# Norm statistics laid out on 128 tokens instead of four column strips (RMS norms) and at full width (layer norms)

## The chip, the cores and the metric

The program runs on one core of a Trainium2 chip. The metric is the device time of one execution in microseconds (us). The core has a matrix engine (PE; its weight loads are listed as PEld), a vector engine (DVE), an activation engine (ACT), a general engine (POOL) and a queue engine (SP) that starts the weight transfers. All data are float32.

## The reference, cut to what matters

The input is a sequence of 512 tokens of width 1024. Two blocks follow each other. The first puts 16 learned tokens in front (528 in all) and normalises four times with a layer norm; the second works on 512 tokens and normalises eight times with an RMS norm:

```
def layer_norm(x, g, b):
    mu = jnp.mean(xf, axis=-1, keepdims=True)
    var = jnp.mean(jnp.square(xf - mu), axis=-1, keepdims=True)
    y = (xf - mu) * lax.rsqrt(var + LN_EPS)
    return y * g + b

def _rmsnorm(x, g):
    y = xf * lax.rsqrt(jnp.mean(xf * xf, axis=-1, keepdims=True) + NORM_EPS)
    return y * g

# first block, 2 layers:   h = layer_norm(ALPHA * h + mixer(h), ...);  h = layer_norm(ALPHA * h + conv_ffn(h), ...)
# second block, 2 layers:  x = x + _rmsnorm(mixer(_rmsnorm(x, g0)), g1);  x = x + _rmsnorm(conv_ffn(_rmsnorm(x, g2)), g3)
```

## The kernel before, in words

Activations lie with the width on the 128 partitions and the tokens along the free axis, as eight tiles of 128 x 528 (or 128 x 512). X is the residual, Z the stream, A the activations. So the mean over the width of one token is a sum over partitions and over eight tiles. The kernel takes it with matmuls against MEANW, a tile filled with 1/1024.

The five engines run programs of their own and meet through semaphores. The order of the work is written out by hand: `when(name, what, n)` gives the semaphore and the value at which the n-th result `what` of the norm `name` is there. In the order of the program the norms are

- lru, ffn0, fox, ffn1: centred (layer norm), 528 tokens, each on the sum of a projection and the residual;
- mixin: RMS, on the residual, at the start of the second block;
- mix, ffn2, gla, ffn3: "out" norms (RMS), on the output of a projection (`rms_out`, which also adds the result to X);
- ffn2in, glain, ffn3in: "in" norms (RMS), on the residual that the out norm has just updated (`rms_in`). ffn2in follows mix, glain follows ffn2, ffn3in follows gla.

A norm has these steps. ACT squares the eight tiles (L2395, in an out norm L2384, where POOL has already added up the first four squares in NORM_MU, so that PE reads five tiles and not eight). PE waits for each square and multiplies it. Before, `squares_of` (L2236) splits the tokens into four strips of 132 or 128; strip g goes with 32 columns of MEANW into rows 32g to 32g+31 of one PSUM bank, four matmuls per tile. ACT takes the root of this 128 x 132 (or 128 x 128) tile (L2397), DVE its reciprocal (L2625), and PE spreads the four strips over all partitions again with four matmuls of one row each (L2250) into four banks. DVE then multiplies the eight tiles by the gain and by these roots in PSUM (L2619 in a layer norm, L2631 in an in norm, L2644 in an out norm). In a layer norm ACT adds the bias and writes X (L2401).

What waits on whom around a norm: the matmuls behind it start with the first normalised tile. POOL's weight combinations of ffn0, ffn1, ffn2 and ffn3 (L2817 to L2825) start as soon as the last centred tile (layer norm) or the last updated X tile (out norm) is there, so for lru, fox, ffn2in and ffn3in they run beside the norm. In ffn2in and ffn3in DVE also makes the combinations of the moving operand (L2543 to L2551) after the multiplications, then two memsets that ACT waits for.

Of the kernel before, what the change touches and what calls it, by code (L numbers as in the profile page):

```python
# [110 lines left out]
def build(nc, x_t, units, cols, gate_w2, out):  # L111
    ctx = ExitStack()
    with ctx:
# [45 lines left out]
        def parts(T):  # L159
            return [(0, 0, HALF), (1, HALF, HALF)] if T == T1 else [(0, 0, T)]  # L160
# [25 lines left out]
        def S(name):  # L186
            if name not in sems:
# [9 lines left out]
        PER = {"mean": 1, "mu": 1, "ctr": KD, "sc": KD, "sq": KD, "zsum": SUMS - 1, "sqsum": SUMS - 1, "var": 1, "std": 1, "rec": 1, "spread": 1, "x": KD,  # L197
               "pad": 1, "tap": 2 * NF, "conv": 2 * NF, "gelu": NF, "act": NF}

        def shared(what, name):  # L200
            return S(("ffn_" if what in ("pad", "tap", "conv", "gelu", "act") else "norm_") + what)

        def when(name, what, n):

            order = (FFNS if what in ("pad", "tap", "conv", "gelu", "act") else SUMMED if what == "sqsum" else
                     NORMS)
            return shared(what, name), n + PER[what] * order.index(name) + (what in ("conv", "act"))

        def credit(eng, *names):
# [2 lines left out]
                eng.sem_inc(S(name), 1)  # L212

        def mean_squares(T):
            return PS[:, 1, 0:T // 4]

        def roots(T):
            return NORM_R[:, 0:T // 4]  # L220

        def root_banks(name):
            return 2 if name == "ffn0" else 4

        def spread_roots(name, T):
            return PS[:, root_banks(name):root_banks(name) + 4, 0:T // 4]

        def by_quarter(ap):
            return ap.rearrange("p (g t) -> p g t", g=4)

        def at_k(name, what):
            return shared(what, name), lambda k: when(name, what, k + 1)[1]
# [1865 lines left out]
        def _(pe):  # L2098
# [118 lines left out]
            def norm(name, T, centred, summed=False):  # L2217

                if centred:

                    pe.wait_ge(tile_free, BUFS + {"lru": TILES["ffn0"], "ffn0": TILES["fox_f"], "fox": TILES["ffn1"], "ffn1": TILES["ssd_pre"]}[name])

                    pe.wait_ge(*when(name, "zsum", SUMS - 1))
                    for b, t, n in parts(T):
                        nc.tensor.matmul(PS[:, 6 + b, 0:n], MEANW[:, 0, :], NORM_MU[:, t:t + n], start=True, stop=False)
                    for k in range(SUMS, KD):
                        pe.wait_ge(q_added, z_ready(name, k))
                        for b, t, n in parts(T):
                            mm = nc.tensor.matmul(PS[:, 6 + b, 0:n], MEANW[:, 0, :], Z[:, k, t:t + n], start=False, stop=(k == KD - 1))
                    mm.then_inc(shared("mean", name), 1)  # L2230
                n = T // 4

                def squares_of(k, tile):
# [4 lines left out]
                    return mm  # L2238

                if summed:  # L2240
                    pe.wait_ge(tile_free, BUFS + {"mix": TILES["ffn2"], "ffn2": TILES["gla_pre"], "gla": TILES["ffn3"], "ffn3": TILES["end"]}[name])
                    pe.wait_ge(*when(name, "sqsum", SUMS - 1))
                    squares_of(0, NORM_MU[:, 0:T])
                for k in range(SUMS if summed else 0, KD):
                    pe.wait_ge(*when(name, "sq", k + 1))
                    mm = squares_of(k, scratch(SQ_AT, KD, T2)[:, k, :] if summed else A[:, k, 0:T])
                mm.then_inc(shared("var", name), 1)
                pe.wait_ge(*when(name, "rec", 1))
                for g in range(4):
                    mm = nc.tensor.matmul(spread_roots(name, T)[:, g, :], ONES[32 * g:32 * g + 1, :], roots(T)[32 * g:32 * g + 1, :],  # L2250
                                          start=True, stop=True)
                mm.then_inc(shared("spread", name), 1)

            def ffn(n, T, h, before):
                name = f"ffn{n}"
# [81 lines left out]
        def _(act):  # L2337
# [48 lines left out]
            def norm(name, T, src, centred, ready, ready_n, eps):  # L2386
                if centred:
                    act.wait_ge(*when(name, "mean", 1))
                    nc.scalar.activation(sv(NORM_MU[:, 0:T], T), ps_tile(6, T), ACT.Copy).then_inc(shared("mu", name), 1)

                spare = 96 + NORMS.index(name)
                nc.scalar.activation(SMALL[:, spare:spare + 1], SMALL[:, eps:eps + 1], ACT.Sqrt)
                for k in range(KD if ready else 0):
                    act.wait_ge(ready, ready_n(k))
                    nc.scalar.activation(A[:, k, 0:T], src(k), ACT.Square).then_inc(shared("sq", name), 1)  # L2395
                act.wait_ge(*when(name, "var", 1))
                nc.scalar.activation(roots(T), mean_squares(T), ACT.Sqrt, bias=SMALL[:, eps:eps + 1]).then_inc(shared("std", name), 1)  # L2397
# [120 lines left out]
        def _(dve):  # L2518
# [92 lines left out]
            def ln(name, g, k0):  # L2611
                dve.wait_ge(*when(name, "mu", 1))
                for k in range(KD):
                    dve.wait_ge(q_added, z_ready(name, k))
                    v.tensor_tensor(Z[:, k, :], Z[:, k, :], NORM_MU[:, :], ALU.subtract).then_inc(shared("ctr", name), 1)
                reciprocal_roots(name, T1)
                for k in range(KD):
                    dve.wait_ge(*when(name, "ctr", k + 1))
                    v.scalar_tensor_tensor(out=by_quarter(Z[:, k, :]), in0=by_quarter(Z[:, k, :]), scalar=col(g, k0 + k),  # L2619
                                           in1=spread_roots(name, T1), op0=ALU.mult, op1=ALU.mult).then_inc(shared("sc", name), 1)  # L2620

            def reciprocal_roots(name, T):

                dve.wait_ge(*when(name, "std", 1))
                v.reciprocal(roots(T), roots(T)).then_inc(shared("rec", name), 1)  # L2625
                dve.wait_ge(*when(name, "spread", 1))

            def rms_in(name, g, into=None):
                reciprocal_roots(name, T2)
                for k in range(KD):  # L2630
                    v.scalar_tensor_tensor(out=by_quarter(Z[:, k, 0:T2]), in0=by_quarter(X[:, k, META:T1]), scalar=col("norm_g", g * 8 + k),  # L2631
                                           in1=spread_roots(name, T2), op0=ALU.mult, op1=ALU.mult).then_inc(shared("x", name), 1)
                    if into is not None and k == KD // 2 - 1:
                        dve.wait_ge(*when(name, "x", KD // 2))
                        moving(CHUNKS[into], 1, KD // 2, lambda k0, k1, a, z: Z[:, k0:k1, a:z], T2 // 2, T2)
                if into is not None:
                    dve.wait_ge(*when(name, "x", KD))
                    for m in range(2, 5):
                        moving(CHUNKS[into], m, KD // 2, lambda k0, k1, a, z: Z[:, k0:k1, a:z], T2 // 2, T2)

            def rms_out(name, g):
                reciprocal_roots(name, T2)
                for k in range(KD):
                    c(v.scalar_tensor_tensor(out=by_quarter(Z[:, k, 0:T2]), in0=by_quarter(Z[:, k, 0:T2]), scalar=col("norm_g", g * 8 + k),  # L2644
                                             in1=spread_roots(name, T2), op0=ALU.mult, op1=ALU.mult))
# [386 lines left out]
```

## Time and profile before

| | us |
|---|---|
| median of 3 runs (3443.97 to 3451.95) | 3444.69 |
| the profiled execution's own time | 3444.69 |
| its span, first to last instruction | 3443.0 |
| PE busy in the span | 3272.9 (95%) |
| DVE / ACT / POOL busy | 1685.1 / 1029.8 / 1138.7 |
| share of PE in the chain that ended last | 88% |

### The profile page before, as it was taken

To read this page: it belongs to the slowest core of one execution; us is meant where nothing else is said; L and a number is where in the kernel's file an instruction comes from. 1 tells how busy PE (TensorE), PEld (TensorE's weight loads), DVE (VectorE), ACT (ScalarE), POOL (GpSimd) and SP (SyncE) were. 2 spreads that over 40 slices of the span, in tenths; PEclk is the share of its full clock that TensorE was granted. 3 is DMA by queue.
4 is the path that set the end of the run, shared out by engine and by line. 5 is a ranking of instruction groups with operands and counts; after the bars stand their busy time and mean duration, and the time that the engine had idled before them with its cause. 6 is when DMAs were issued, how large, how long until landed. Compare 5 with 4: busy or idle time off the path is not lost.

```text
span 3443.0 us, 51186 instructions
## 1 busy us (share of the span) xinstructions
PE 3272.9 (95%) x16742; PEld 2647.2 (77%) x16742; DVE 1685.1 (49%) x2837; ACT 1029.8 (30%) x2083; POOL 1138.7 (33%) x920
## 2 busy tenths in 40 slices
PE   9999999989999999998999999989999899799997
PEld 7787888867776788886446787868888588688886
DVE  3454546454445354644546545354553534355544
ACT  3433232122332223212317333122321334222311
POOL 0024444432221344442001333344444222353543
PEclk9999999999999999997999999989999899899999
DMA  3222222211111122221210211212222221122222
GB/s 119 82 83 92 79 91 79 92 68 50 56 50 38 68 79 91 79 92 49 68 55 21 67 55 55 70 65 91 79 92 80 67 68 62 49 73 89 88 89 76
DMA packets 68669, 249.35 MB, mean 72 GB/s; under 512 B 7568, under 2 KB 7568, under 8 KB 68544
## 3 DMA queue, kind: packets, MB, share of 16 engines
q1 hardware_dynamic: 68544, 247.72, 20.9%
q8 instruction: 74, 1.21, 0.1%
q14 instruction: 51, 0.42, 0.0%
HBM read 245.59 MB, written 2.10 MB: 72 GB/s over the span
## 4 chain that ended last, share of the span: by engine, by line
PE 88%; DVE 6%; ACT 3%; issue 2%; DVEq 0%; POOL 0%; DMA 0%; ACTq 0%; SPq 0%; POOLq 0%
PE psum L2188 54%; PE psum L2123 10%; PE psum L431 6%; PE psum L1742 3%; PE psum L1300 3%; PE psum L1327 1%; PE psum L1767 1%; PE psum L463 1%; PE psum L2288 1%; PE psum L1354 1%; PE psum L501 1%; DVE residual L2646 1%; DVE stream L2644 1%; ACT scratch L1033 1%; PE psum L485 1%
## 5 line engine op out<-in xcount | busy, mean ns | idle before, releaser
L2188 PE MATMUL psum<-scratch 128*128 128x256 f32 (+1 forms) x3600 | 817.1, 383 | 11.3 <-POOL scratch L2820 5.8
L2188 PEld LDWEIGHTS psum<-scratch 128*128 128x128 f32 x3600 | 684.8, 190 | 119.4 <-ACT scratch L2354 7.9
L2817 POOL TENSOR_TENSOR scratch<-w_ring 128x512 f32<-128x512 f32 (+2 forms) x160 | 201.7, 1261 | 1366.1 <-DMA w_ring<-units 806.3
L2354 ACT ACTIVATE scratch<-psum 128x264 f32<-128x264 f32 (+1 forms) x480 | 184.5, 386 | 889.8 <-PE psum L2188 863.1
L2669 DVE TENSOR_TENSOR scratch<-scratch,psum 128x264 f32<-128x264 f32 (+1 forms) x264 | 108.3, 424 | 502.9 <-PE psum L2188 475.0
L2188 PE MATMUL psum<-scratch,w_ring 128*128 128x256 f32 (+1 forms) x1200 | 275.6, 382 | 0.0
L2188 PEld LDWEIGHTS psum<-scratch,w_ring 128*128 128x128 f32 x1200 | 227.9, 190 | 34.9
L2188 PE MATMUL psum<-acts,w_ring 128*128 128x264 f32 (+1 forms) x1088 | 247.8, 386 | 2.6 <-ACT scratch L2469 1.1
L2188 PEld LDWEIGHTS psum<-acts,w_ring 128*128 128x128 f32 x1088 | 208.0, 192 | 35.9 <-issue 2.6
L2417 ACT ACTIVATE scratch<-scratch,params 128x528 f32<-128x528 f32 (+1 forms) x176 | 144.4, 821 | 274.9 <-DVE scratch L2669 274.9
L2822 POOL TENSOR_TENSOR scratch<-w_ring 128x512 f32<-128x512 f32 (+2 forms) x160 | 225.9, 1412 | 0.0
L2825 POOL TENSOR_TENSOR scratch<-w_ring,scratch 128x512 f32<-128x512 f32 (+2 forms) x160 | 224.7, 1405 | 2.9 <-PE psum L2188 2.9
L2820 POOL TENSOR_TENSOR scratch<-scratch,w_ring 128x512 f32<-128x512 f32 (+2 forms) x160 | 219.5, 1372 | 12.5
L2676 DVE SCALAR_TENSOR_TENSOR scratch<-scratch,params 128x528 f32<-128x528 f32 (+1 forms) x176 | 201.6, 1145 | 25.5 <-DVE scratch L2674 9.0
L2674 DVE SCALAR_TENSOR_TENSOR scratch<-scratch,params 128x528 f32<-128x528 f32 (+1 forms) x176 | 204.2, 1160 | 0.0
L2123 PE MATMUL psum<-residual,w_ring 128*128 128x264 f32 (+1 forms) x800 | 181.1, 389 | 6.2 <-DMA residual<-x_t 6.2
L2123 PE MATMUL psum<-stream,w_ring 128*128 128x512 f32 (+1 forms) x400 | 179.6, 604 | 1.0 <-DVE stream L2631 1.0
L2123 PEld LDWEIGHTS psum<-residual,w_ring 128*128 128x128 f32 (+1 forms) x800 | 149.5, 188 | 37.3 <-issue 8.2
L2188 PE MATMUL psum<-residual,w_ring 128*128 128x264 f32 x704 | 165.3, 394 | 3.5 <-ACT residual L2401 3.5
L2188 PE MATMUL psum<-stream,w_ring 128*128 128x256 f32 x704 | 159.9, 386 | 1.9 <-DVE stream L2631 1.9
L2188 PEld LDWEIGHTS psum<-residual,w_ring 128*128 128x128 f32 x704 | 137.0, 195 | 28.2 <-issue 3.9
L2188 PEld LDWEIGHTS psum<-stream,w_ring 128*128 128x128 f32 x704 | 136.6, 194 | 21.7 <-issue 2.5
(456 smaller groups left out, 4760.3 us busy)
## 6 DMA issues: line engine op xcount, KB each, us to landing
w_ring<-units SPq DMA_DIRECT2D x463, 512.0 KB, 3.6
residual<-x_t SPq DMA_DIRECT2D x4, 528.0 KB, 6.5
out_t<-residual SPq DMA_DIRECT2D x4, 512.0 KB, 2.7
params<-cols SPq DMA_DIRECT2D x1, 568.5 KB, 8.5
gate_w_sb<-gate_w SPq DMA_DIRECT2D x1, 96.0 KB, 10.5
```

What stands on the lines that cost most here:

```text
L431: mm = nc.tensor.matmul(fx_bank(p), weights(k), moving(k), start=(p in (1, 2, 5) and k == 0), stop=(k == 3), skip_group_check=True)
L2123: mm = nc.tensor.matmul(PS[0:m1 - m0, bank + b, 0:n], W[:, s, q, m0:m1], rhs(k)[:, t:t + n], start=(k == 0), stop=(k == slots[-1][1] + slo ...
L2188: mm = nc.tensor.matmul(out, weights(k), moving(k), start=(p in (1, 2, 5) and k == 0), stop=(k == h - 1), skip_group_check=(p != 2))
L2354: nc.scalar.activation(kept(q, n, H), quad_bank(q, p, H), ACT.Copy).then_inc(q_copied, 1)
L2417: nc.scalar.activation(y[:, j, 0:T], xp[:, j, 0:T], ACT.Identity, bias=w(3), scale=w(0)).then_inc(shared("tap", name), 1)
L2669: v.tensor_tensor(xp[:, row, at:at + H], kept(q, keep, H), quad_bank(q, p, H), ALU.add).then_inc(q_added, 1)
L2674: c(v.scalar_tensor_tensor(out=y[:, j, 0:T], in0=xp[:, j, 1:1 + T], scalar=PAR[:, ds(w0 + 1, 1)], in1=y[:, j, 0:T], op0=ALU.mult, op1=ALU. ...
L2676: v.scalar_tensor_tensor(out=y[:, j, 0:T], in0=xp[:, j, 2:2 + T], scalar=PAR[:, ds(w0 + 2, 1)], in1=y[:, j, 0:T], op0=ALU.mult, op1=ALU.ad ...
L2817: g.tensor_tensor(s(1), row(1, 0), row(1, 1), ALU.add).then_inc(q_weight, 1)
L2820: g.tensor_tensor(s(2), s(1), row(0, 0), ALU.subtract).then_inc(q_weight, 1)
L2822: g.tensor_tensor(s(3), row(0, 0), row(1, 0), ALU.subtract).then_inc(q_weight, 1)
L2825: g.tensor_tensor(s(4), row(0, 1), s(2), ALU.subtract).then_inc(q_weight, 1)
```

## The change

RMS norms (512 tokens). The squares become the stationary operand: for each block of 128 tokens, `squares_of` multiplies the 128 x 128 block of squares with one column of MEANW, so that the mean of token p of block j stands in row p of column j. The result is 128 x 4, added over the tiles. ACT takes the root of 128 x 4, DVE its reciprocal (into SMALL), and then DVE makes four diagonal matrices (identity times one column of roots, "diag"), and PE multiplies them with ONES into one bank, which gives the roots of 512 tokens on all partitions. The multiplications read this bank.

Layer norms (528 tokens). PE multiplies each square with all 128 columns of MEANW in two halves of 264 tokens, so that all partitions hold the variance. ACT takes the root of 128 x 528, DVE the reciprocal of 128 x 528 in SBUF, and the multiplications read that. There is no spreading matmul.

```
-                for g in range(4):
-                    mm = nc.tensor.matmul(mean_squares(T)[32 * g:32 * g + 32], MEANW[:, 0, 0:32], tile[:, n * g:n * g + n],
-                                          start=(k == 0), stop=(k == KD - 1), skip_group_check=True)
...
-                pe.wait_ge(*when(name, "rec", 1))
-                for g in range(4):
-                    mm = nc.tensor.matmul(spread_roots(name, T)[:, g, :], ONES[32 * g:32 * g + 1, :], roots(T)[32 * g:32 * g + 1, :], start=True, stop=True)
+                if T == T2:
+                    def squares_of(k, tile):
+                        for j in range(T2 // P):
+                            mm = nc.tensor.matmul(rms_v[:, j:j + 1], tile[:, P * j:P * j + P], MEANW[:, 0, 0:1], start=(k == 0 and j == 0), stop=True, skip_group_check=True)
...
+                    for j in range(T2 // P):
+                        pe.wait_ge(*when(name, "diag", j + 1))
+                        mm = nc.tensor.matmul(rms_r[:, P * j:P * j + P], ONES[:, :], NORM_R[:, P * j:P * j + P], start=True, stop=True)
...
+                for k in range(KD):
+                    pe.wait_ge(*when(name, "sq", k + 1))
+                    for b, t, n in parts(T):
+                        mm = nc.tensor.matmul(PS[:, 6 + b, 0:n], MEANW[:, 0, :], A[:, k, t:t + n], start=(k == 0), stop=(k == KD - 1))
...
-                nc.scalar.activation(roots(T), mean_squares(T), ACT.Sqrt, bias=SMALL[:, eps:eps + 1])
+                if T == T2:
+                    nc.scalar.activation(rms_t, rms_v, ACT.Sqrt, bias=SMALL[:, eps:eps + 1])
+                    return
+                nc.scalar.activation(sv(NORM_R[:, 0:T], T), ps_tile(6, T), ACT.Sqrt, bias=SMALL[:, eps:eps + 1])
...
+                c(v.reciprocal(NORM_R[:, :], NORM_R[:, :]))
...
-                    v.scalar_tensor_tensor(out=by_quarter(Z[:, k, :]), in0=by_quarter(Z[:, k, :]), scalar=col(g, k0 + k), in1=spread_roots(name, T1), ...)
+                    v.scalar_tensor_tensor(out=Z[:, k, :], in0=Z[:, k, :], scalar=col(g, k0 + k), in1=NORM_R[:, :], ...)
...
+            def rms(name):
+                dve.wait_ge(*when(name, "std", 1))
+                c(v.reciprocal(rms_t, rms_t))
+                for j in range(T2 // P):
+                    v.tensor_scalar(NORM_R[:, P * j:P * j + P], ID[:, :], rms_t[:, j:j + 1], None, ALU.mult).then_inc(shared("diag", name), 1)
+                dve.wait_ge(*when(name, "spread", 1))
```

On PE, at the norms ffn1 (a layer norm) and mixin (an RMS norm), which follow each other, the program has before (the size is the rows and columns of the output):

```order
L2229 MATMUL psum<-stream,mean_weights 128x264 x8
L2236 MATMUL psum<-acts,mean_weights 32x132 x32
L2250 MATMUL psum<-norm_r,ones 128x132 x4
L2236 MATMUL psum<-acts,mean_weights 32x128 x32
L2250 MATMUL psum<-norm_r,ones 128x128 x4
L789 MATMUL psum<-w_ring,stream 128x64 x32
```

and after the change:

```order
L2215 MATMUL psum<-stream,mean_weights 128x264 x8
L2241 MATMUL psum<-acts,mean_weights 128x264 x16
L2221 MATMUL psum<-mean_weights,acts 128x1 x32
L2235 MATMUL psum<-norm_r,ones 128x128 x4
L775 MATMUL psum<-w_ring,stream 128x64 x32
```

The layer norm has sixteen matmuls of 264 columns for its 32 short ones and no spreading matmuls; the RMS norm has as many matmuls as before, each of one column with a new 128 x 128 stationary operand.

On PE, at the norms mix (out) and ffn2in (in), between the projection and the next feed-forward part, the program has before:

```order
L2236 MATMUL psum<-norm_mu,mean_weights 32x128 x4
L2236 MATMUL psum<-scratch,mean_weights 32x128 x16
L2250 MATMUL psum<-norm_r,ones 128x128 x4
L2236 MATMUL psum<-acts,mean_weights 32x128 x32
L2250 MATMUL psum<-norm_r,ones 128x128 x4
```

and after the change:

```order
L2221 MATMUL psum<-mean_weights,norm_mu 128x1 x4
L2221 MATMUL psum<-mean_weights,scratch 128x1 x16
L2235 MATMUL psum<-norm_r,ones 128x128 x4
L2221 MATMUL psum<-mean_weights,acts 128x1 x32
L2235 MATMUL psum<-norm_r,ones 128x128 x4
```

Nothing has changed its place; the forms have changed.

On DVE, at ffn1 and mixin, before:

```order
L2615 TENSOR_TENSOR stream<-stream,norm_mu 128x528 x8
L2625 RECIPROCAL norm_r<-norm_r 128x132
L2619 SCALAR_TENSOR_TENSOR stream<-stream,params,psum 128x528 x8
L2625 RECIPROCAL norm_r<-norm_r 128x128
L2631 SCALAR_TENSOR_TENSOR stream<-residual,params,psum 128x512 x8
```

and after the change:

```order
L2608 TENSOR_TENSOR stream<-stream,norm_mu 128x528 x8
L2610 RECIPROCAL norm_r<-norm_r 128x528
L2613 SCALAR_TENSOR_TENSOR stream<-stream,params,norm_r 128x528 x8
L2619 RECIPROCAL small<-small 128x4
L2621 TENSOR_SCALAR norm_r<-identity,small 128x128 x4
L2627 SCALAR_TENSOR_TENSOR stream<-residual,params,psum 128x512 x8
```

The layer norm's reciprocal is four times as wide and its multiplications read no PSUM; the RMS norm's reciprocal has four columns, and four operations that build diagonals stand behind it.

## Rows read from the trace of the kernel before

**Rows 1.** The page: the span, and the chain that ended last by engine.

```profile
span 3443.0 us, 51186 instructions
...
PE 88%; DVE 6%; ACT 3%; issue 2%; DVEq 0%; POOL 0%; DMA 0%; ACTq 0%; SPq 0%; POOLq 0%
```

**Rows 2.** Timeline of the norm lru: start, duration, engine, line, operation, count, idle before.

```profile
297.24 3.72 PE L2229 MATMUL psum<-stream,mean_weights 128*128 128x264 f32 x16
...
303.71 4.42 PE L2236 MATMUL psum<-acts,mean_weights 128*32 128x132 f32 x64 [2.75 <-ACT acts L2395]
...
308.19 0.37 ACT L2397 ACTIVATE norm_r<-psum,small 128x132 f32<-128x132 f32 x1 [0.79 <-PE psum L2236]
...
308.60 0.98 DVE L2625 RECIPROCAL norm_r<-norm_r 128x132 f32<-128x132 f32 x1 [1.92 <-ACT norm_r L2397]
...
310.52 5.49 DVE L2619 SCALAR_TENSOR_TENSOR stream<-stream,params,psum 128x528 f32<-128x528 f32 x8 [0.94 <-PE psum L2250]
...
315.90 1.27 POOL L2825 TENSOR_TENSOR scratch<-w_ring,scratch 128x512 f32<-128x512 f32 x1
```

**Rows 3.** Groups by line and form: DVE reciprocals and ACT roots; busy us, mean ns.

```profile
L1190 DVE RECIPROCAL scratch<-scratch 128x512 f32<-128x512 f32 x2 | 6.7, 3344 | 0.0
...
L2030 DVE RECIPROCAL scratch<-scratch 128x4 f32<-128x4 f32 x4 | 0.7, 178 | 27.7 <-ACT scratch L1935 27.7
```

```profile
L1484 ACT ACTIVATE scratch<-scratch,small 128x4 f32<-128x4 f32 x8 | 2.4, 297 | 0.1
...
L1044 ACT ACTIVATE scratch<-psum,small 128x512 f32<-128x512 f32 x2 | 1.4, 687 | 2.9 <-PE psum L956 2.9
```

**Rows 4.** Stretches: us, then busy (count) of each engine, granted clock, DMA share, GB/s.

```profile
735.60:740.00 4.40, 4.19 (x64) 1.55 (x64) 3.05 (x5) 3.79 (x8) 0.00 (x0) 0.61 0.02 4
...
1611.40:1615.70 4.30, 4.28 (x64) 1.59 (x64) 0.00 (x0) 3.60 (x7) 0.00 (x0) 0.50 0.01 4
...
2273.90:2284.30 10.40, 5.24 (x64) 1.60 (x64) 8.76 (x13) 4.41 (x7) 1.05 (x1) 0.50 0.01 2
...
2287.50:2292.70 5.20, 5.14 (x12) 4.20 (x13) 5.17 (x8) 0.00 (x0) 5.12 (x4) 0.50 0.00 0
```

**Rows 5.** Stretches of L821, then of L789: busy of PE and PEld, granted clock.

```profile
1656.60:1659.50 2.90, 2.63 (x24) 2.76 (x24) 1.00 0.00 0
```

```profile
1623.50:1634.30 10.80, 10.80 (x51) 10.74 (x50) 0.50 0.00 0
```

**Rows 6.** Timeline of the out norms mix, then ffn2.

```profile
2266.91 0.43 PE L2236 MATMUL psum<-norm_mu,mean_weights 128*32 128x128 f32 x8
...
2269.73 0.37 ACT L2397 ACTIVATE norm_r<-psum,small 128x128 f32<-128x128 f32 x1 [0.45 <-PE psum L2236]
...
2271.71 0.75 DVE L2644 SCALAR_TENSOR_TENSOR stream<-stream,params,psum 128x512 f32<-128x512 f32 x1 [0.63 <-PE psum L2250]
```

```profile
2692.73 0.43 PE L2236 MATMUL psum<-norm_mu,mean_weights 128*32 128x128 f32 x8
...
2696.44 0.35 ACT L2397 ACTIVATE norm_r<-psum,small 128x128 f32<-128x128 f32 x1
```

**Rows 7.** Timeline of the in norm ffn2in.

```profile
2273.90 0.65 PE L2236 MATMUL psum<-acts,mean_weights 128*32 128x128 f32 x8 [2.26 <-ACT acts L2395]
...
2283.25 1.26 POOL L2817 TENSOR_TENSOR scratch<-w_ring 128x512 f32<-128x512 f32 x1 [17.51 <-DVE residual L2646]
...
2283.58 0.66 PE L2236 MATMUL psum<-acts,mean_weights 128*32 128x128 f32 x8 [0.72 <-ACT acts L2395]
...
2286.66 2.72 DVE L2631 SCALAR_TENSOR_TENSOR stream<-residual,params,psum 128x512 f32<-128x512 f32 x4 [0.94 <-PE psum L2250]
...
2293.31 2.01 DVE L2546 TENSOR_TENSOR scratch<-stream,scratch 128x1024 f32<-128x1024 f32 x1
```

**Rows 8.** Timeline between 770 and 775 us, where DVE and POOL alternate.

```profile
770.78 0.48 DVE L651 TENSOR_SCALAR scratch<-scratch,identity 16x528 f32<-16x528 f32 x1
...
771.30 1.38 DVE L652 TENSOR_SCALAR scratch<-scratch,identity 16x528 f32<-16x528 f32 x1
772.47 1.34 POOL L724 TENSOR_TENSOR scratch<-scratch,w_ring 128x512 f32<-128x512 f32 x1
```

More of the change, by code:

```diff
@@ L196, in build @@
         SUMS = KD // 2
-        PER = {"mean": 1, "mu": 1, "ctr": KD, "sc": KD, "sq": KD, "zsum": SUMS - 1, "sqsum": SUMS - 1, "var": 1, "std": 1, "rec": 1, "spread": 1, "x": KD,
+        PER = {"mean": 1, "mu": 1, "ctr": KD, "sc": KD, "sq": KD, "zsum": SUMS - 1, "sqsum": SUMS - 1, "var": 1, "std": 1, "diag": T2 // P, "spread": 1, "x": KD,
                "pad": 1, "tap": 2 * NF, "conv": 2 * NF, "gelu": NF, "act": NF}
@@ L205, in when @@
             order = (FFNS if what in ("pad", "tap", "conv", "gelu", "act") else SUMMED if what == "sqsum" else
-                     NORMS)
+                     NORMS[4:] if what in ("diag", "spread") else NORMS)
             return shared(what, name), n + PER[what] * order.index(name) + (what in ("conv", "act"))
@@ L212, in credit @@
                 eng.sem_inc(S(name), 1)
[L216 to L229, printed above, removed]
+        rms_v, rms_t, rms_r = PS[:, 7, 300:300 + T2 // P], SMALL[:, 140:140 + T2 // P], PS[:, 6, 0:T2]
         def at_k(name, what):
@@ L2230, in norm @@
                     mm.then_inc(shared("mean", name), 1)
-                n = T // 4
-                def squares_of(k, tile):
-                    for g in range(4):
-                        mm = nc.tensor.matmul(mean_squares(T)[32 * g:32 * g + 32], MEANW[:, 0, 0:32], tile[:, n * g:n * g + n],
-                                              start=(k == 0), stop=(k == KD - 1), skip_group_check=True)
[L2238 to L2243, printed above, removed]
@@ L2244, in norm @@
-                for k in range(SUMS if summed else 0, KD):
+                if T == T2:
+                    def squares_of(k, tile):
+                        for j in range(T2 // P):
+                            mm = nc.tensor.matmul(rms_v[:, j:j + 1], tile[:, P * j:P * j + P], MEANW[:, 0, 0:1], start=(k == 0 and j == 0),
+                                                  stop=True, skip_group_check=True)
+                        return mm
+                    if summed:
+                        pe.wait_ge(tile_free, BUFS + {"mix": TILES["ffn2"], "ffn2": TILES["gla_pre"], "gla": TILES["ffn3"], "ffn3": TILES["end"]}[name])
+                        pe.wait_ge(*when(name, "sqsum", SUMS - 1))
+                        squares_of(0, NORM_MU[:, 0:T])
+                    for k in range(SUMS if summed else 0, KD):
+                        pe.wait_ge(*when(name, "sq", k + 1))
+                        mm = squares_of(k, scratch(SQ_AT, KD, T2)[:, k, :] if summed else A[:, k, 0:T])
+                    mm.then_inc(shared("var", name), 1)
+                    for j in range(T2 // P):
+                        pe.wait_ge(*when(name, "diag", j + 1))
+                        mm = nc.tensor.matmul(rms_r[:, P * j:P * j + P], ONES[:, :], NORM_R[:, P * j:P * j + P], start=True, stop=True)
+                    mm.then_inc(shared("spread", name), 1)
+                    return
@@ L2252, in norm @@
-                mm.then_inc(shared("spread", name), 1)
             def ffn(n, T, h, before):
@@ L2396, in norm @@
                 act.wait_ge(*when(name, "var", 1))
-                nc.scalar.activation(roots(T), mean_squares(T), ACT.Sqrt, bias=SMALL[:, eps:eps + 1]).then_inc(shared("std", name), 1)
+                if T == T2:
+                    nc.scalar.activation(rms_t, rms_v, ACT.Sqrt, bias=SMALL[:, eps:eps + 1]).then_inc(shared("std", name), 1)
+                    return
+                nc.scalar.activation(sv(NORM_R[:, 0:T], T), ps_tile(6, T), ACT.Sqrt, bias=SMALL[:, eps:eps + 1]).then_inc(shared("std", name), 1)
                 if centred:
@@ L2615, in ln @@
                     v.tensor_tensor(Z[:, k, :], Z[:, k, :], NORM_MU[:, :], ALU.subtract).then_inc(shared("ctr", name), 1)
[L2616 removed]
+                dve.wait_ge(*when(name, "std", 1))
+                c(v.reciprocal(NORM_R[:, :], NORM_R[:, :]))
                 for k in range(KD):
                     dve.wait_ge(*when(name, "ctr", k + 1))
[L2619 to L2622 removed]
+                    v.scalar_tensor_tensor(out=Z[:, k, :], in0=Z[:, k, :], scalar=col(g, k0 + k), in1=NORM_R[:, :],
+                                           op0=ALU.mult, op1=ALU.mult).then_inc(shared("sc", name), 1)
+            def rms(name):
                 dve.wait_ge(*when(name, "std", 1))
[L2625 removed]
+                c(v.reciprocal(rms_t, rms_t))
+                for j in range(T2 // P):
+                    v.tensor_scalar(NORM_R[:, P * j:P * j + P], ID[:, :], rms_t[:, j:j + 1], None, ALU.mult).then_inc(shared("diag", name), 1)
                 dve.wait_ge(*when(name, "spread", 1))
             def rms_in(name, g, into=None):
[L2629 removed]
+                rms(name)
                 for k in range(KD):
[L2631 to L2632 removed]
+                    v.scalar_tensor_tensor(out=Z[:, k, 0:T2], in0=X[:, k, META:T1], scalar=col("norm_g", g * 8 + k),
+                                           in1=rms_r, op0=ALU.mult, op1=ALU.mult).then_inc(shared("x", name), 1)
                     if into is not None and k == KD // 2 - 1:
@@ L2641, in rms_out @@
             def rms_out(name, g):
-                reciprocal_roots(name, T2)
+                rms(name)
                 for k in range(KD):
-                    c(v.scalar_tensor_tensor(out=by_quarter(Z[:, k, 0:T2]), in0=by_quarter(Z[:, k, 0:T2]), scalar=col("norm_g", g * 8 + k),
-                                             in1=spread_roots(name, T2), op0=ALU.mult, op1=ALU.mult))
+                    c(v.scalar_tensor_tensor(out=Z[:, k, 0:T2], in0=Z[:, k, 0:T2], scalar=col("norm_g", g * 8 + k),
+                                             in1=rms_r, op0=ALU.mult, op1=ALU.mult))
                     v.tensor_tensor(X[:, k, META:T1], X[:, k, META:T1], Z[:, k, 0:T2], ALU.add).then_inc(shared("x", name), 1)
```

3 lines of the change are left out of this document (removed).

## The prediction

> **What bounds the kernel now.** I read the page first, then the chain of waits, then the timeline around each of the twelve norms, then the groups by line and form for the prices of the new operations, and last the granted clock of single stretches. The page's chain is 88% PE [rows 1]: the kernel is a long row of matmuls, and only where PE waits can an edit outside of the matmuls tell. The norms are such places. In the timeline of the norm lru the reader is to see one file of short steps, each waiting for the one ahead: the last squares' matmuls end at 308.13, root at 308.19, reciprocal at 308.60, first multiplication at 310.52 [rows 2]. Nothing else is ready for PE in that time, and the next products need the normalised tiles. The same file stands in all twelve norms. So whatever a norm gets longer from its first square to its first multiplication is added to the whole time. The profiled execution took 3444.69 us, which is the median of the three runs, against a span of 3443.0 [rows 1]; I add my sum to 3444.7.
>
> **Layer norms, variance on PE (four: lru, ffn0, fox, ffn1).** Before, 64 records take 4.42 us [rows 2], as long as ACT takes to deliver the squares. After, there are 16 matmuls of 264 columns with 128 columns of weights, 32 records. The mean just ahead has this very form: 16 records in 3.72 us at the full clock, so 32 take 7.44. PE, not ACT, is the slower now: +3.0 us. In lru and ffn1 I take the full clock, since the work that keeps PE busy starts again at 303.7. In ffn0 the granted clock was 0.61 over 4.4 us [rows 4], which is 3.4 us at half, and fox shows the same; there half the rate for 3.4 us costs another 1.7, and the 9.15 stands against 4.3: +4.85. Sum 2 x 3.0 + 2 x 4.85 = 15.7. Bounds: 12.2 (all at the full clock), 19 (3.4 us at half in all four).
>
> **Layer norms, from variance to first multiplication.** The root of 528 columns out of PSUM: 0.69 after the row of 512 [rows 3] against 0.37 [rows 2], +0.32. The reciprocal: 3344 ns for 512 columns [rows 3] and 0.98 us for 132 [rows 2] lie on one line of 6.2 ns a column, so 528 take 3.44, +2.46. The spreading falls away: 0.94 from the end of the reciprocal (309.58) to 310.52 [rows 2], against about 0.05 for DVE's own wait. Net +1.9 each, 7.6 for four. The multiplications themselves cost what they did, one per 0.69 us, and ACT behind them keeps its pace.
>
> **DVE beside POOL in layer norms.** The multiplications now read only SBUF, and POOL still works on weights: in lru until 317.2 [rows 2]. The first multiplication would come at about 315.5, so that one or two of them meet POOL. L652 took 1.38 us beside POOL where the like L651 took 0.48 [rows 8], so 0.9 is the price of one meeting; with one in lru and one in fox, 1.8. Bounds: 0 and some 5.
>
> **RMS norms, the dot products.** Here is the largest part. Each tile now needs four matmuls with a fresh 128 x 128 stationary operand and one moving column, so the eight weight loads set the time and not the columns. Two lines of before show such work: L821 (8 columns) with 24 loads in 2.76 us at clock 1.00, 0.115 each; L789 (64 columns) with 50 in 10.74 at 0.50, 0.215 each [rows 5]. A tile costs 0.92 us at the full clock and 1.72 at half.
> - mixin: the clock is 0.50 [rows 4], the squares come every 0.53 us. Eight tiles take 13.8 against 4.3: +9.5. At the full clock 7.4: +3.1.
> - ffn2in, glain, ffn3in: the squares come every 1.38 us, because DVE makes them one by one, and the clock is 0.50 [rows 4]. Before, PE had time left. At 1.72 a tile it has none: 13.8 from 2273.90, against 10.34 to the end of the last group [rows 7]. +3.45 each, 10.4. At the full clock only the last tile shows, +0.26 each.
> - out norms, five tiles: PE comes from dense work at the full clock. I take 4 us of full clock and then half, so 5.3 in all (4.3 tiles, then 0.7 at 1.72). In mix the root started at 2269.73 [rows 6]; after 2266.91 + 5.3 it starts at 2272.2, +2.5, and gla is built alike. In ffn2 and ffn3 ACT loads a table for the root, which hid PE's end: root at 2696.44 [rows 6], after 2692.73 + 5.3 + 0.06, +1.65. Sum 8.3. Bounds: 5.6 (full clock, 4.6 us), 21.6 (half throughout, 8.6 us).
>
> **A rule on the clock.** The row of L789 has PE busy for 10.8 us without a gap at 0.50 [rows 5]. The Trainium skill ("TensorE: Matmul & The Clock Gate", section "What's actually happening") says that throttled is the default state and activity releases it. By that rule 13.8 us of unbroken work in a norm should bring the full clock, and the sum would be that of the first rival below. This trace speaks against it for work that is mostly weight loads.
>
> **RMS norms, from dot products to first multiplication.** Before: 2.42 us in ffn2in (2284.24 to 2286.66) [rows 7], 2.03 in mix [rows 6]. After, at half clock: 0.06 + root 0.30 + 0.08 + reciprocal 0.18 [rows 3] + 0.03; the first diagonal 0.29, my estimate for 128 columns from L651's 0.48 for 528 [rows 8] and a fixed part; then PE with four matmuls, eight loads at 0.215 = 1.72, and some 0.33 for its pipeline and the hand-overs: 2.99. So the seven-fold cheaper reciprocal buys nothing: its 0.77 us goes into four diagonals and full 128-row matmuls where four one-row matmuls ran beside each other. mixin and glain +0.57 each, 1.1; four out norms +0.95 each, 3.8. At the full clock the chain takes 2.4: 0 and +0.4.
>
> **The diagonals beside POOL (ffn2in, ffn3in).** The wait for "diag" is new, and what is queued behind it is PE's spreading and then every product of the feed-forward part. POOL starts its eight operations at 2283.25 [rows 7], each 1.26 to 1.27 long, so it works until about 2293.4; the four diagonals would come at 2288. Where both want SBUF they alternate: DVE's 0.48 became 1.38 [rows 8]. Four diagonals at 1.38 take 5.5 and the chain 7.0 instead of 2.42: +4.6. In exchange POOL is done by the time that DVE makes its combinations: L2546's 2.01 us [rows 7] is 1.2 alone, and this chain sets ACT's start, -0.8. Net +3.8, twice: 7.6. Bounds: -0.2 and 4.6 each.
> The Trainium skill ("SBUF — State Buffer", section "Who interferes with whom") says that a DVE instruction with at most one SBUF input outside of the two-port modes does not contend with GpSimd, while `tensor_scalar` can enter such a mode and then holds the shared pair, the other side blocked. By the first half the diagonals pass unhindered and the sum is that of the second rival; rows 8 show the second half.
>
> **Sum.** 15.7 + 7.6 + 1.8 + 9.5 + 10.4 + 8.3 + 1.1 + 3.8 + 7.6 = 65.8 us, so 3510.5, call it 3511. Nothing of it lies beside other work, for the reason of the first paragraph. No transfer is moved: SP is ahead with the weights in every norm.
>
> **Rivals.**
> 1. *The full clock holds through the norms.* For it: lru keeps 1.00 for 5 us past the dense work, and the new work leaves no gaps on PE. Against it: L789's row. Then layer norms 12.2 + 7.6 + 1.8, mixin 3.1, in norms 0.8, out norms 5.6, chains 0 + 1.6, diagonals beside POOL 7.2: 39.9, time 3485.
> 2. *No meeting with POOL.* For it: 128 columns are short, and a diagonal may slip in between two POOL operations. Against it: rows 8. The two terms 1.8 and 7.6 become 0 and -0.5: 3501. With the first rival as well, 3476.
> 3. *Not slower.* One-column matmuls with hidden weight loads cost no more than before, the chain gains the 0.77 of the reciprocal in eight norms (6.2), and the clock stays full past the norms: L789's 10.8 us [rows 5] shrinks by 5, and five stretches like 2287.50 to 2292.70 at 0.50 [rows 4] by 2.6 each, 13. Against the layer norms' 12.2 + 7.6 this gives -4.4: 3440. It decides from the point where a 128-column load costs below about 0.06 us at the granted clock; nothing in the trace is below 0.115.
>
> **How the numbers follow.** The forecast 0.66, rival 1 0.18, rival 2 0.14, rival 3 0.02. The range goes from both first rivals together (3476) to the forecast with the out norms wholly at half clock (+13.3) and half clock in lru and ffn1 (+3.4): 3476 to 3528. A measurement of this kernel can tell about 0.3% (10.3 us) from no change. All cases but the last lie above that: slower 0.96, same 0.02, faster 0.02.
>
> **What would show it.** In the profile after: the sixteen variance matmuls about 7.4 to 9.2 us from the first to the last; a reciprocal of 128x528 at 3.4; the 128x1 matmuls of an in norm spread over 13.8 us at clock 0.50, with PE no longer idle between them; about 3.0 us from the last of them to the first multiplication in mixin, and 7 in ffn2in with diagonals at 1.38. I am wrong if the 128x1 groups take 0.9 us or less per tile at 0.50, if the clock in 2274 to 2288 is 1.00, or if a gap that I took to be PE's alone closes elsewhere.

## The result, and the profile after

The changed kernel takes 3507.8 us (median of 4 runs, 3507.1 to 3511.0) against 3444.3 for the kernel before in the same session: +63.4 us, a ratio of 1.0182 with a 95% interval of 1.0165 to 1.0200. Forecast were 3511 and +65.8.

The page of the changed kernel, to be put beside [rows 1]; the span is 63.6 us longer:

```profile
span 3506.6 us, 50898 instructions
...
PE 90%; DVE 5%; issue 2%; ACT 2%; DVEq 0%; POOL 0%; DMA 0%; ACTq 0%; SPq 0%; POOLq 0%
```

PE's part of the chain has grown from 88 to 90%, though nothing was added to the products. The timeline of the norm lru in the changed kernel answers to [rows 2] (start, duration, engine, line):

```profile
304.96 9.07 PE L2241 MATMUL psum<-acts,mean_weights 128*128 128x264 f32 x32 [2.75 <-ACT acts L2385]
...
314.07 0.70 ACT L2390 ACTIVATE norm_r<-psum,small 128x528 f32<-128x528 f32 x1 [5.43 <-PE psum L2241]
...
314.81 3.45 DVE L2610 RECIPROCAL norm_r<-norm_r 128x528 f32<-128x528 f32 x1 [6.88 <-ACT norm_r L2390]
...
317.13 1.26 POOL L2821 TENSOR_TENSOR scratch<-w_ring,scratch 128x512 f32<-128x512 f32 x1
318.30 5.52 DVE L2613 SCALAR_TENSOR_TENSOR stream<-stream,params,norm_r 128x528 f32<-128x528 f32 x8
```

The squares' matmuls last 9.07 us instead of 4.42, the reciprocal 3.45 instead of 0.98. POOL ends at 318.39, when the first multiplication begins: the two don't meet, and the eight multiplications take 5.52 as against 5.49.

In fox, the other layer norm with POOL beside it, they do meet. The kernel before, then the changed one:

```profile
1172.71 5.49 DVE L2619 SCALAR_TENSOR_TENSOR stream<-stream,params,psum 128x528 f32<-128x528 f32 x8 [0.63 <-PE psum L2250]
1173.59 1.28 POOL L2825 TENSOR_TENSOR scratch<-w_ring,scratch 128x512 f32<-128x512 f32 x1
```

```profile
1188.33 1.26 POOL L2818 TENSOR_TENSOR scratch<-w_ring 128x512 f32<-128x512 f32 x1
1189.03 6.89 DVE L2613 SCALAR_TENSOR_TENSOR stream<-stream,params,norm_r 128x528 f32<-128x528 f32 x8
1189.55 1.73 POOL L2821 TENSOR_TENSOR scratch<-w_ring,scratch 128x512 f32<-128x512 f32 x1
```

Before, the multiplications read the roots in PSUM and took 5.49 us with POOL working beside them. Now they read only SBUF. The first takes 1.12 us and the second 1.77, where the later ones take 0.76, and the first product starts 2.04 us behind the first multiplication and not 1.67.

The timeline of the norm ffn2in, to [rows 7]:

```profile
2313.84 13.81 PE L2221 MATMUL psum<-mean_weights,acts 128*128 128x1 f32 x64 [2.23 <-ACT acts L2385]
...
2327.69 0.27 ACT L2388 ACTIVATE small<-psum,small 128x4 f32<-128x4 f32 x1 [4.22 <-PE psum L2221]
...
2328.06 0.18 DVE L2619 RECIPROCAL small<-small 128x4 f32<-128x4 f32 x1 [5.25 <-ACT small L2388]
...
2328.27 3.90 DVE L2621 TENSOR_SCALAR norm_r<-identity,small 128x128 f32<-128x128 f32 x4
...
2333.06 2.72 DVE L2627 SCALAR_TENSOR_TENSOR stream<-residual,params,psum 128x512 f32<-128x512 f32 x4 [0.89 <-PE psum L2235]
...
2339.71 1.22 DVE L2539 TENSOR_TENSOR scratch<-stream,scratch 128x1024 f32<-128x1024 f32 x1
```

PE runs without a gap for 13.81 us where it had been idle for half of the time, and four diagonals take 3.90 us beside POOL. One by one (four narrow windows of the same timeline):

```profile
2328.27 1.28 DVE L2621 TENSOR_SCALAR norm_r<-identity,small 128x128 f32<-128x128 f32 x1
2329.47 0.28 DVE L2621 TENSOR_SCALAR norm_r<-identity,small 128x128 f32<-128x128 f32 x1
2329.66 1.29 DVE L2621 TENSOR_SCALAR norm_r<-identity,small 128x128 f32<-128x128 f32 x1
2330.87 1.30 DVE L2621 TENSOR_SCALAR norm_r<-identity,small 128x128 f32<-128x128 f32 x1
```

The second starts at the end of one POOL operation (2329.46), before the next (2329.54), and takes no longer than alone. In mixin, where POOL is idle, four take 0.87:

```profile
1650.23 0.87 DVE L2621 TENSOR_SCALAR norm_r<-identity,small 128x128 f32<-128x128 f32 x4
1650.57 1.78 PEld L2235 LDWEIGHTS psum<-norm_r,ones 128*128 128x128 f32 x8 [1.04 <-DVE norm_r L2621]
1650.57 2.08 PE L2235 MATMUL psum<-norm_r,ones 128*128 128x128 f32 x8 [0.96 <-DVE norm_r L2621]
```

The granted clock (the third number from the right) in stretches of the changed kernel, from the first to the last variance matmul of lru, ffn0, mixin, mix and gla:

```profile
304.96:314.03 9.07, 9.07 (x32) 7.18 (x32) 2.97 (x5) 3.68 (x7) 5.63 (x5) 0.81 0.00 0
744.12:751.51 7.39, 7.39 (x32) 6.00 (x32) 2.98 (x5) 3.68 (x7) 0.00 (x0) 1.00 0.00 0
...
1635.79:1649.60 13.81, 13.81 (x64) 13.73 (x64) 0.00 (x0) 3.59 (x7) 0.00 (x0) 0.50 0.00 1
2304.13:2308.65 4.52, 4.52 (x41) 4.43 (x39) 0.85 (x2) 1.89 (x5) 0.00 (x0) 1.00 0.02 4
3047.10:3053.15 6.05, 6.05 (x41) 5.97 (x39) 0.42 (x1) 1.43 (x4) 0.00 (x0) 0.72 0.01 3
```

Read for all twelve norms in both traces, the two intervals of the path are (us, before and after):

| norm | first square on PE to root | root to first multiplication | sum of both |
|---|---|---|---|
| lru | 4.48, 9.11 | 2.33, 4.23 | +6.5 |
| ffn0 | 4.37, 7.43 | 2.02, 4.22 | +5.3 |
| fox | 4.25, 7.43 | 2.02, 4.22 | +5.4 |
| ffn1 | 4.48, 9.11 | 2.32, 4.22 | +6.5 |
| mixin | 4.36, 13.86 | 2.35, 3.03 | +10.2 |
| mix | 2.82, 4.56 | 1.98, 2.97 | +2.7 |
| ffn2in | 10.40, 13.85 | 2.36, 5.37 | +6.5 |
| ffn2 | 3.71, 5.17 | 1.96, 2.96 | +2.5 |
| glain | 10.41, 13.86 | 2.35, 3.03 | +4.1 |
| gla | 2.36, 6.09 | 2.29, 2.97 | +4.4 |
| ffn3in | 10.40, 13.85 | 2.36, 5.39 | +6.5 |
| ffn3 | 3.71, 5.72 | 2.27, 2.97 | +2.7 |

They add up to 63.3 of the 63.6 us. Outside of these intervals single stretches shift too: 2.8 us less from ffn0 to fox, 1.5 more from fox to ffn1, 2.7 more from mixin to mix, 1.7 less from glain to gla. They come to less than half a us in all; that they cancel is luck, and their causes were not looked into one by one.

### The profile page after: what moved, and what is told of

It reads as the page before. It is cut to its first block, busy times and chain, and to the rows that moved or that the text cites. A ratio compares the mean times of both kernels' runs of the same rounds, so it can differ in the third digit from the quotient of the medians.

```text
span 3506.6 us, 50898 instructions
## 1 busy us (share of the span) xinstructions
PE 3348.2 (95%) x16582; PEld 2745.0 (78%) x16582; DVE 1709.1 (49%) x2869; ACT 1031.5 (29%) x2083; POOL 1137.2 (32%) x920
## 4 chain that ended last, share of the span: by engine, by line
PE 90%; DVE 5%; issue 2%; ACT 2%; DVEq 0%; POOL 0%; DMA 0%; ACTq 0%; SPq 0%; POOLq 0%
PE psum L2174 53%; PE psum L2109 10%; PE psum L417 6%; PE psum L1728 3%; PE psum L1286 2%; PE psum L2221 2%; PE psum L1313 1%; PE psum L1753 1%; PE psum L2278 1%; PE psum L449 1%; PE psum L1340 1%; PE psum L2241 1%; PE psum L487 1%; ACT scratch L1019 1%; PE psum L471 1%
## 5 line engine op out<-in xcount | busy, mean ns | idle before, releaser
L2174 PEld LDWEIGHTS psum<-residual,w_ring 128*128 128x128 f32 x704 | 136.9, 195 | 38.4 <-issue 13.0
```

The costliest lines, as they stand in the source:

```text
L2174: mm = nc.tensor.matmul(out, weights(k), moving(k), start=(p in (1, 2, 5) and k == 0), stop=(k == h - 1), skip_group_check=(p != 2))
```

## The experiments

Each was timed in 4 runs beside the kernel before on the same chip, which stood at 3447.3 for the first four kernels below and at 3446.9 for the last four. I compare distances from the kernel before: +63.4 for the changed kernel. Each distance has an interval of some 6 us to either side, so a difference of a few us between two of them is shown only by the profiles.

**Half of the change: RMS norms only.** The layer norms are those of before.

```
-                    for b, t, n in parts(T):
-                        mm = nc.tensor.matmul(PS[:, 6 + b, 0:n], MEANW[:, 0, :], A[:, k, t:t + n], ...)
+                    for g in range(4):
+                        mm = nc.tensor.matmul(mean_squares(T)[32 * g:32 * g + 32], MEANW[:, 0, 0:32], A[:, k, n * g:n * g + n], ...)
```

> The changed RMS norms with the layer norms of before. Theory: the 63 us are the sum of twelve separate lengthenings, and the layer norms hold 23.7 of them (6.5, 5.3, 5.4, 6.5 between first square on PE and first multiplication). Then this kernel is at before + 39.6, about 3484, and mixin costs +10.2, ffn2in and ffn3in +6.5 each, glain +4.1 as in the changed kernel. Rival: the two halves act on each other through the clock (a layer norm's dense matmuls or its longer wait decide the clock that the RMS norms see) or through what is hidden behind them; then the two single halves do not add up to 63 within 4 us.

Measured: 3485.7, +38.4, ratio 1.0106 (1.0089 to 1.0123). In its profile mixin has lost 10.2 us, ffn2in and ffn3in 6.5 each and glain 4.1, as in the changed kernel. The out norms moved with the clock: mix took 6.5 us to the root at a clock of 0.67, where it has 4.6 at 1.00 in the changed kernel.

**The other half: layer norms only.**

> The changed layer norms with the RMS norms of before. Theory: before + 23.7, about 3468, made of 3.0 to 4.7 us more from first square to root in each norm (sixteen matmuls of 264 columns instead of 32 short ones) and 2.0 more from root to first multiplication (reciprocal of 528 columns 3.45 us). Rival as for the other half: with it the sum of the two differs from 63 by more than 4.

Measured: 3470.8, +23.5, ratio 1.0061 (1.0043 to 1.0080). The two halves make 61.9 of 63.4: they add up, within what the intervals allow; these are too wide to exclude the 4 us of the rival, which the profiles have to do. In this one mixin, mix, ffn2in, glain and ffn3in keep the times of before to 0.02 us; in the layer norms only the clock moves (ffn0 and fox took 9.1 and 8.9 to the root here, 7.4 in the changed kernel).

**One weight load pair a tile instead of four.**

```
-                        for j in range(T2 // P):
-                            mm = nc.tensor.matmul(rms_v[:, j:j + 1], tile[:, P * j:P * j + P], MEANW[:, 0, 0:1], ...)
+                        return nc.tensor.matmul(rms_v, tile[:, 0:P], MEANW[:, 0, 0:4], ...)
```

> The changed kernel with one matmul of four columns per tile of squares instead of four of one column, all with the first 128 tokens as stationary operand: the mean squares of the other 384 tokens are left out, the rest is as it was. Theory: the weight loads are the price of the RMS dot products (0.215 us each at the half clock, eight a tile). With two loads a tile PE has time left, and the terms of the dot products go: 9.5 in mixin, 3.45 in each of three in norms, 8.9 in the four out norms, 28.8 in all: about 3479. In mixin the eight tiles end 4.3 to 4.5 us after the first. Rival: a fixed price of each wait for a square and of the half clock; then mixin's 13.8 us fall by little.

Measured: 3479.8, +32.5, ratio 1.0092 (1.0073 to 1.0112): 30.9 less than the changed kernel. The timeline of its mixin, at the same clock of 0.50:

```profile
1635.13 4.23 PE L2220 MATMUL psum<-mean_weights,acts 128*128 128x4 f32 x16 [11.21 <-ACT acts L2382]
```

4.23 us for eight tiles, the pace of the squares. So the clock of 0.50 by itself costs nothing there, nor do the waits. This kernel has fewer matmuls as well as fewer loads, and can't tell one from the other; the kernel before can. Its mixin had four matmuls a tile at the same clock, with weights 32 columns wide:

```profile
1611.42 0.20 PEld L2236 LDWEIGHTS psum<-acts,mean_weights 128*32 128x32 f32 x8 [7.30 <-ACT acts L2395]
1611.42 4.29 PE L2236 MATMUL psum<-acts,mean_weights 128*32 128x128 f32 x64 [6.99 <-ACT acts L2395]
```

Eight of its loads take 0.20 us, and PE keeps up with the squares. As many matmuls with 128-column loads take 1.72: the loads are the price. Of the twelve norms in this trace, the eight RMS norms lost 27.0 us together; ffn2in and ffn3in lost less than their 3.5, since their diagonals now came 3.5 us earlier into POOL's work (6.27 us from root to first multiplication).

**One dense matmul more per tile.** In ffn2in, glain and ffn3in:

```
+                        if not summed and name != "mixin":
+                            nc.tensor.matmul(PS[:, 4, 0:256], MEANW[:, 1, :], A[:, k, 0:256], start=True, stop=True)
```

> The changed kernel with one more matmul of 256 columns (result unused, into a free bank) ahead of each tile's four in ffn2in, glain and ffn3in. Theory: the in norms run at the half clock because nearly no columns move, and at the full clock a tile would take 0.92 us and be hidden behind the squares that come every 1.38. If 256 columns a tile bring the full clock, the tile takes 0.92 + 0.22, PE catches up with the squares and each of the three norms loses about 3 us although PE does more: about 3499. Rival (the clock is not raised by it, or has no part in the cost): a tile takes 1.72 + 0.43 = 2.15, each of the three norms gets 3.4 longer: about 3518.

Measured: 3527.2, +79.9, ratio 1.0223 (1.0206 to 1.0240). My theory falls in the form that it had: with 256 more columns a tile the clock stays at 0.50 through the norm, and eight tiles take 19.6 us. The rival's 3518 is missed too, since it had priced a tile at 2.15 us and it took 2.45:

```profile
2316.20:2335.80 19.60, 19.60 (x79) 18.28 (x77) 7.78 (x12) 4.12 (x7) 9.91 (x8) 0.50 0.00 1
```

The same run had something that I hadn't expected of it: with the norm that much later, POOL had ended its eight operations, and root to first multiplication fell from 5.37 to 3.03 in ffn2in and from 5.39 to 3.04 in ffn3in. In glain, where POOL is idle, it stayed at 3.04. So the long diagonals go with POOL's operations and not with the place.

**Two dense matmuls of 512 columns more per tile.**

> The changed kernel with two more matmuls of 512 columns (results unused) ahead of each tile's four in ffn2in, glain and ffn3in, where one of 256 did not raise the clock. Theory: the clock goes by the columns that move, not by PE being occupied with weight loads; with 1024 extra columns of float32 a tile the granted clock in these norms is 1.00 after its first microseconds, the four matmuls with their loads take 0.92 and the fillers 1.8, so 2.7 a tile and about 22 us a norm, +8 each against the changed kernel: about 3532. Rival: the clock stays at 0.50 whatever is added; then a tile takes 1.7 + 3.6 and each norm 42, about 3590.

Measured: 3533.4, +86.4, ratio 1.0260 (1.0243 to 1.0277), close to the forecast of about 3532. PE's work in its ffn2in begins at 2312.65. The granted clock in the last 6.8 us before 2322.00 and in the 16 us behind it:

```profile
2315.21:2322.00 6.79, 6.79 (x19) 4.05 (x17) 6.24 (x10) 3.02 (x6) 0.00 (x0) 0.51 0.00 0
2322.00:2338.00 16.00, 16.00 (x77) 10.26 (x76) 0.00 (x0) 0.28 (x1) 9.91 (x8) 1.00 0.00 1
```

and one tile of it at the full clock:

```profile
2327.61 1.96 PE L2233 MATMUL psum<-acts,mean_weights 128*128 128x512 f32 x4
2329.41 0.95 PE L2221 MATMUL psum<-mean_weights,acts 128*128 128x1 f32 x8
```

At 1.00 the four one-column matmuls take 0.95 instead of 1.71, and the chain behind them 2.1 instead of 3.0. So the half clock does nearly double the price of the loads, and in the changed kernel mixin, ffn2in, glain and ffn3in stayed at it; but the full clock, bought with extra matmuls, costs more than it gives. What about the extra matmuls raised it the two kernels don't tell: they differ in columns, in number and in length.

**Diagonals on ACT.** DVE only takes the reciprocal:

```
-                    v.tensor_scalar(NORM_R[:, P * j:P * j + P], ID[:, :], rms_t[:, j:j + 1], None, ALU.mult) ...
+                        nc.scalar.activation(NORM_R[:, P * j:P * j + P], ID[:, :], ACT.Copy, scale=rms_t[:, j:j + 1]) ...
```

> The changed kernel with the four diagonals made by ACT (identity times a column of roots as scale) and not by DVE. Theory: the 5.37 us from root to first multiplication in ffn2in and ffn3in, against 3.0 in the six other RMS norms, come from DVE's diagonals alternating with POOL's operations on SBUF; ACT doesn't meet POOL, so both fall to about 3.1, and all others stay at 3.0 plus 0.1 for the hop: between 3 and 5 us less than the changed kernel, about 3504. Rival: the price is one of the place (ACT's table load behind the root, or weights that PE needs from POOL); then ffn2in and ffn3in stay above 5.

Measured: 3505.7, +58.7, ratio 1.0171 (1.0154 to 1.0188), 4.7 less than the changed kernel. The intervals overlap, and the two profiled spans are alike (3506.7 and 3506.6), with ffn0, for one, 1.7 longer at a lower clock here; that the whole kernel gains is not shown. What the profile does show is the norm itself. In ffn2in POOL works throughout:

```profile
2330.00 1.26 POOL L2822 TENSOR_TENSOR scratch<-w_ring,scratch 128x512 f32<-128x512 f32 x1
...
2331.22 1.26 POOL L2814 TENSOR_TENSOR scratch<-w_ring 128x512 f32<-128x512 f32 x1
2331.27 1.28 ACT L2391 ACTIVATE norm_r<-identity,small 128x128 f32<-128x128 f32 x4 [0.31 <-DVE small L2622]
```

Four diagonals take 1.28 us there, root to first multiplication is 3.14 in ffn2in and 3.15 in ffn3in, and 3.07 to 3.14 in the six others. The rival (table load, weights) is out: it had them above 5.

**A short reciprocal in the layer norms.** `NORM_R[:, 0:132]` in place of all 528 columns.

> The changed kernel with the layer norms' reciprocal over 132 of the 528 columns only: for the other 396 tokens the multiplication is by the root itself. Theory: the reciprocal costs 6.2 ns a column on the path of every layer norm, so each gets 2.47 us shorter from root to first multiplication (4.22 to 1.75) and the kernel 9.9: about 3498. Rival: POOL's weights or another engine would be late next, and part of it does not come back; then the products behind the norm start later than the first normalised tile.

Measured: 3496.8, +49.9, ratio 1.0155 (1.0134 to 1.0176), 13.5 less than the changed kernel. In the profile root to first multiplication is 1.74 or 1.75 in all four layer norms, 2.48 less, as expected. Not all of it arrives. In lru and fox the multiplications now come earlier into POOL's work:

```profile
315.50 7.55 DVE L2613 SCALAR_TENSOR_TENSOR stream<-stream,params,norm_r 128x528 f32<-128x528 f32 x8
1183.15 8.82 DVE L2613 SCALAR_TENSOR_TENSOR stream<-stream,params,norm_r 128x528 f32<-128x528 f32 x8
```

They had taken 5.52 and 6.89 in the changed kernel. From the first multiplication to the next norm it is 1.1 us longer behind lru and 1.5 behind fox, so as far as these stretches tell about half of their 5.0 is given back: the rival was right in part, though the engine that came late is DVE. The kernel gained as much as forecast all the same, since ffn2, gla and ffn3 took 2.1 us less to the root together and other stretches between the norms were 2.9 shorter; that is the clock in the three norms, and was not looked into in the stretches. (ffn1 got 7.4 to the root instead of 9.1, and ffn0 9.1 instead of 7.4.)

**Half of the layer norms' variance.**

```
-                    for b, t, n in parts(T):
+                    for b, t, n in parts(T) if k == 0 else parts(T)[:1]:
...
```

> The changed kernel with the squares of tiles 1 to 7 multiplied for the first 264 tokens only: the layer norms' variance of the other 264 tokens counts tile 0 alone. Theory: PE is the slower in the layer norms' variance; with one matmul of 264 columns a tile (0.46 us at the full clock against a square every 0.54) it is hidden again, and the stretch from first square to root falls from 7.4 to 9.1 to 4.6 to 5.1, so 13 to 15 us less than the changed kernel, about 3494. Rival: the stretch is set by the half clock that comes with any gap; then a tile takes 0.93 and the stretch stays at 7.4 or more.

Measured: 3496.2, +49.2, ratio 1.0145 (1.0128 to 1.0162), 14.2 less than the changed kernel. To the root it takes 6.0 in lru and ffn0, at a clock of 0.71 (more than the 4.6 to 5.1 expected), and 4.48 in fox and ffn1 at 1.00, where it was 7.4 to 9.1. The rival's 7.4 or more is out. Here too the multiplications of lru and fox come into POOL's work, and take 8.10 and 9.27 us. The matmuls of ffn1 show gaps again, waiting for ACT's squares, so PE was the slower by its own work:

```profile
1610.44 4.45 PE L2241 MATMUL psum<-acts,mean_weights 128*128 128x264 f32 x18 [2.75 <-ACT acts L2385]
1613.64 0.30 PEld L2241 LDWEIGHTS psum<-acts,mean_weights 128*128 128x128 f32 x2 [0.23 <-ACT acts L2385]
```

## Why the prediction was right, term by term

| term | forecast | measured in the profile |
|---|---|---|
| layer norms, variance | 15.7 | 15.5 |
| layer norms, root to first multiplication | 7.6 | 8.2 |
| layer norms, DVE beside POOL | 1.8 | 0 in lru, 0.4 to 1.4 in fox |
| mixin, dot products | 9.5 | 9.5 |
| in norms, dot products | 10.4 | 10.4 |
| out norms, dot products | 8.3 | 8.9 |
| mixin and glain, chain behind | 1.1 | 1.4 |
| out norms, chain behind | 3.8 | 3.4 |
| diagonals beside POOL, and what follows | 7.6 | 6.0 less 1.5 |

The mechanism came out as forecast; that the sum is within 2.4 us owes something to luck, since errors of parts cancelled in the layer norms' variance and in the out norms, and the shifts between the norms cancelled too.

- *The variance of the layer norms* came out right in sum and wrong in its parts. I gave lru and ffn1 the full clock and ffn0 and fox 3.4 us at half; it was the other way round, 0.81 in lru and ffn1 (9.07 us) and 1.00 in ffn0 and fox (7.39). The experiments show both values in the same norm with the same work (ffn0 has 9.11 with one load pair a tile and 7.4 here), so from these traces a forecast can only say 7.4 or 9.1.
- *The line through two reciprocals* (6.2 ns a column) gave 3.44; measured 3.45. The short reciprocal shows that it lay on the way to the first multiplication wholly.
- *The dot products.* The price per load at half clock, read from L789, was 0.215; 64 loads took 13.73 to 13.81 us. That PE, not DVE, would pace the in norms followed from 1.72 against 1.38 a tile, and the kernel with one load pair confirms it from the other side. The out norms are right in sum and wrong in parts: five tiles took 4.52 us at 1.00 in mix and 6.05 at 0.72 in gla, where I had taken 5.3 for both, so that mix lost 1.7 and gla 3.7 instead of 2.5 each.
- *The rival of the full clock* did not come true: 0.50 in mixin, ffn2in, glain and ffn3in. The rule that activity releases the throttle (the Trainium skill, "TensorE: Matmul & The Clock Gate", section "What's actually happening") doesn't bring the full clock here: PE was occupied for 13.81 us without a gap, by loads and one-column matmuls, and stayed at 0.50. Of the two kernels that put dense matmuls between them, the one with 256 columns stayed at 0.50 too and the one with two matmuls of 512 rose to 1.00. Whoever had read the 13.8 us of unbroken work by that rule would have forecast the first rival's 3485.
- *The rival "not slower"* asked for a 128-column load below about 0.06 us. The shortest pace in the changed kernel is that of mix at the full clock, 39 loads in 4.43 us, 0.114 each.
- *DVE beside POOL.* The mechanism was right in ffn2in and ffn3in, its size too large: I priced each of four diagonals at 1.38, in sum 5.5, and they took 3.90: three paid 1.28 to 1.30, and the second slipped between two operations of POOL, which was my second rival's argument and held for one in four. The chain cost +3.0 each and not +4.6. What comes back later is as forecast: L2539 takes 1.22 where L2546 had 2.01, and the first product on the combined operand starts 10.78 us behind the first multiplication instead of 11.55. In the layer norms I had one meeting each in lru and fox. In lru the longer variance (9.07 where I had 7.44) moved DVE to POOL's end, and it cost nothing. In fox DVE met POOL, and the eight multiplications took 1.4 us longer; the first product was 0.4 later. This lies outside of the twelve intervals, so their 63.3 us don't hold it. One multiplication that meets POOL takes 1.77 instead of 0.76, so 1.0 a meeting where I had 0.9.
- *Nothing hid anything.* The assumption under the sum was that a norm's length goes into the time one to one. 63.3 of 63.6 us stand in the twelve intervals, and the three experiments that shortened them by much (one load pair, short reciprocal, half variance) gave back 30.9, 13.5 and 14.2 us. It is not one to one where POOL still works behind the norm, as the short reciprocal shows in lru and fox.

The layout that the change brings makes root and reciprocal cheap (0.27 and 0.18 us on 128 x 4) and pays with four full weight loads per tile and four diagonals: 3.0 us from root to first multiplication where 2.0 to 2.4 had been. The kernel before stays the faster one in each of the twelve norms, and no experiment pointed to a mixture that beats it.

## What to carry to other kernels

A matmul with one moving column and a fresh 128 x 128 stationary operand is priced by its weight loads; count those, at the granted clock of the place where they stand, and compare with the pace of the engine that feeds it. Before an operation on few columns is traded against one on many, look which of them lies on a path where nothing else runs: here a reciprocal over four times as many columns cost 2.5 us in each of four norms, and a reciprocal over 4 columns saved 0.8 that its new neighbours spent. Count small DVE operations that read and write SBUF at their price beside POOL if POOL works then: four diagonals took 3.90 us and not 0.87. And operands that move from PSUM to SBUF can bring an engine into such a meeting, as the multiplications of fox show (6.89 us for 5.49).

## What the runs showed of the hardware that I had not expected

- PE fully occupied with weight loads and 256 moving float32 columns a tile (2.45 us) stood at 0.50 (1.2 GHz) for the whole 19.6 us of a norm; with 1024 columns a tile it stood at 0.51 in ffn2in until 9.4 us behind the norm's first matmul, and at 1.00 (2.4 GHz) from there.
- ACT builds four 128 x 128 diagonals in 1.28 us while POOL works, where DVE takes 3.90; without POOL DVE's four take 0.87.
- Multiplications with one operand in PSUM took 5.49 us beside POOL in fox; with all operands in SBUF they took 6.89, and POOL's operation beside them 1.73 instead of 1.27.
